# A state-space mixer in two blocks on one core: the order of GpSimd's two jobs in the decay matrix, and the slots of two exponentials

## The reference

```
z, xbc, dt = split(u @ w_in)
xbc = silu(dwconv(xbc, conv_w, conv_b)); xh, bm, cm = split(xbc)
# per chunk, for each of the two directions:
cum = cumsum(dt * a)
decay = exp(where(causal, cum[:, None] - cum[None], -inf))
y = einsum(cb * decay, xdt)                         # inside the chunk
y += einsum(c, state) * exp(cum)                    # from the chunks before
state = state * exp(cum[-1]) + einsum(b, xdt * tail)
# both directions and the skip, then
y = rmsnorm_per_group(y * silu(z)) @ w_out
```

## Time and profile before

| | us |
|---|---|
| median of 3 runs | 1842.42 |
| lowest, highest | 1839.36, 1845.85 |
| the profiled execution | 1839.35 |
| its span | 1837.6 |

### The profile page before, as it was taken

One profiled execution on the slowest core, in us unless ns is written; L12 is line 12 of the kernel. 1 busy time (PEld: TensorE's weight loads), 2 busy tenths in 40 slices (PEclk: granted clock), 3 DMA queues, 4 the chain that ended last, 5 costly groups with the idle time before them and its releaser, 6 DMA issues.

```text
span 1837.6 us, 20988 instructions
## 1 busy us (share of the span) xinstructions
PE 1703.0 (93%) x7944; PEld 1368.1 (74%) x7944; DVE 1107.7 (60%) x1520; ACT 842.0 (46%) x1365; POOL 362.3 (20%) x299
## 2 busy tenths in 40 slices
PE   6878898898887999999998899999999999999998
PEld 4766676686665768888776677888678778888886
DVE  6666666667576757574747666776655653434343
ACT  5655565465543453444445235446354442414232
POOL 0253434444354000000004401222120110000001
PEclk9989999999998999999999999999999999999999
DMA  3633443443321222222222223222323233333331
GB/s 103 177 118 96 116 130 103 126 114 103 93 72 48 81 58 80 70 72 78 69 59 85 68 65 74 63 68 80 102 81 104 83 89 102 93 98 98 93 102 69
DMA packets 260106, 164.58 MB, mean 90 GB/s; under 512 B 26909, under 2 KB 249286, under 8 KB 258982
## 3 DMA queue, kind: packets, MB, share of 16 engines
q1 hardware_dynamic: 260006, 163.25, 31.0%
HBM read 160.86 MB, written 2.36 MB: 89 GB/s over the span
## 4 chain that ended last, share of the span: by engine, by line
PE 65%; DVE 12%; issue 9%; ACT 6%; POOL 5%; DMA 2%; SPq 1%; ACTq 0%; POOLq 0%; DVEq 0%
PE stream L79 18%; PE stream L81 18%; PE stream L80 18%; ACT weights_hi L137 2%; DVE weights_lo L147 2%; POOL ssd_work L726 2%; PE q L775 1%; DVE ssd_x L980 1%; PE q L1962 1%; PE q L1986 1%; DMA ssd_exp_cum<-ssd_cum_pairs 1%; POOL ssd_work L730 1%; PE q L79 1%; PE q L81 1%; PE q L80 1%
## 5 line engine op out<-in xcount | busy, mean ns | idle before, releaser
L79 PE MATMUL stream<-u_lo,weights_hi 128*128 128x512 f32 (+2 forms) x1312 | 532.2, 406 | 11.5 <-DVE u_lo L249 4.5
L80 PE MATMUL stream<-u_hi,weights_lo 128*128 128x512 f32 (+2 forms) x1312 | 515.2, 393 | 0.0
L81 PE MATMUL stream<-u_hi,weights_hi 128*128 128x512 f32 (+2 forms) x1312 | 515.2, 393 | 0.0
L137 ACT ACTIVATE weights_hi<-weights_raw 128x1024 fp32r<-128x1024 f32 (+4 forms) x269 | 268.7, 1001 | 499.1 <-PE stream L81 473.1
L147 DVE TENSOR_TENSOR weights_lo<-weights_raw,weights_hi 128x1024 fp32r<-128x1024 f32 (+4 forms) x269 | 323.2, 1203 | 278.0 <-ACT weights_hi L137 277.7
L79 PEld LDWEIGHTS stream<-u_lo,weights_hi 128*128 128x128 f32 (+2 forms) x1312 | 248.2, 189 | 77.9 <-issue 9.3
L80 PEld LDWEIGHTS stream<-u_hi,weights_lo 128*128 128x128 f32 (+2 forms) x1312 | 247.9, 189 | 54.6 <-issue 4.9
L81 PEld LDWEIGHTS stream<-u_hi,weights_hi 128*128 128x128 f32 (+2 forms) x1312 | 247.4, 189 | 55.2 <-issue 0.7
L217 POOL COPY h_sum_of_squares<-h_squares 128x512 f32<-128x512 f32 x5 | 3.2, 649 | 795.3 <-ACT h_squares L205 795.3
L79 PE MATMUL stream<-ssd_y_lo,weights_hi 128*128 128x512 f32 x128 | 61.0, 477 | 45.2 <-DVE ssd_x L980 33.2
L79 PE MATMUL stream<-mlp_a_lo,weights_hi 128*128 128x512 f32 x256 | 100.2, 391 | 0.0
(11 more groups left out here) (460 smaller groups left out, 2925.6 us busy)
## 6 DMA issues: line engine op xcount, KB each, us to landing
weights_raw<-in_w_mlp_dram SPq DMA_DIRECT2D x64, 512.0 KB, 3.8
weights_raw<-in_ssd_w_in_dram SPq DMA_DIRECT2D x48, 512.0 KB, 4.1
weights_raw<-in_gla_w_in_dram SPq DMA_DIRECT2D x40, 512.0 KB, 3.8
ssd_cum_steps<-ssd_cum_rows SPq DMA_DIRECT2D x32, 512.0 KB, 4.9
weights_raw<-in_w_in_dram SPq DMA_DIRECT2D x29, 512.0 KB, 3.8
ssd_exp_cum<-ssd_cum_pairs SPq DMA_DIRECT2D x16, 512.0 KB, 7.6
weights_raw<-in_ssd_w_out_dram SPq DMA_DIRECT2D x16, 512.0 KB, 3.6
weights_raw<-in_gla_w_out_dram SPq DMA_DIRECT2D x13, 512.0 KB, 3.4
```

What stands on the lines that cost most here:

```text
L79: pe.matmul(out, lh, rl, start=first, stop=False, skip_group_check=skip)
L80: pe.matmul(out, ll, rh, start=False, stop=False, skip_group_check=skip)
L81: return pe.matmul(out, lh, rh, start=False, stop=last, skip_group_check=skip)
L137: act.activation(w_view(c, n)[0], raw_view(c, n), ACT.Copy).then_inc(c.w_rounded, 1)
```

## The change

POOL's joins get a table of their own, `JOIN`, one slot behind the cuts (for group 0: slots 0 and 1 of round 1; for the others slots 4, 5, 6 and 7). In a slot, the joins now stand behind the work; only in slot 7 do they stand ahead of `complete`. ACT's exponentials of the joined steps (`DECAY`) each come one slot later. The exponentials of `ex` move from slots 2 and 5 to slots 4 and 5. No instruction is added or taken away.

```diff
--- before.py
+++ after.py
@@ -598,12 +598,13 @@
         G = range(SG)
         CONV = {2: 0, 3: 1, 5: 2, 6: 3}
         CUT = {(0, 7): ((0, 0), (0, 1)), (1, 0): ((0, 2), (0, 3))}
-        DECAY = {(1, 0): ((0, 0), (0, 1)), (1, 1): ((0, 2), (0, 3))}
+        JOIN = {(1, 0): ((0, 0), (0, 1)), (1, 1): ((0, 2), (0, 3))}
+        DECAY = {(1, 1): ((0, 0), (0, 1)), (1, 2): ((0, 2), (0, 3))}
         for g in range(1, SG):
-            for t, cut, decay in ((0, (g, 3), (g, 4)), (1, (g, 4), (g, 5)), (2, (g, 5), (g, 6)),
-                                   (3, (g, 6), (g + 1, 0))):
-                CUT[cut] = CUT.get(cut, ()) + ((g, t),)
-                DECAY[decay] = DECAY.get(decay, ()) + ((g, t),)
+            for t, cut, join, decay in ((0, (g, 3), (g, 4), (g, 5)), (1, (g, 4), (g, 5), (g, 6)),
+                                        (2, (g, 5), (g, 6), (g + 1, 0)), (3, (g, 6), (g, 7), (g + 1, 1))):
+                for table, slot in ((CUT, cut), (JOIN, join), (DECAY, decay)):
+                    table[slot] = table.get(slot, ()) + ((g, t),)
 
         def conv_tile(g, j):
             return (2 * g, 2 * g + 1, 2 * SG + g, 3 * SG + g)[j]
@@ -700,17 +701,21 @@
                 pool.wait_ge(s_zsilu, g + 1)
                 pool.tensor_tensor(y[:, p, :], y[:, p, :], zs[:, g % 2, p, :], ALU.mult).then_inc(s_fin, 1)
 
+            def join_steps(i, k):
+                for pg, t in JOIN.get((i, k), ()):
+                    pool.wait_ge(s_cut, 4 * pg + t + 1)
+                    flat_steps = [steps[:, (4 * pg + t) % RING, d, :, :].rearrange("p h l -> p (h l)") for d in range(2)]
+                    pool.tensor_tensor(flat_steps[0], flat_steps[0], flat_steps[1], ALU.add).then_inc(s_join, 1)
+
             for i, k in slots:
                 g = i - 1
                 if k == 0 and i - 2 in G:
                     complete(i - 2, 1)
-                for pg, t in CUT.get((i, k), ()):
-                    pool.wait_ge(s_cut, 4 * pg + t + 1)
-                    flat_steps = [steps[:, (4 * pg + t) % RING, d, :, :].rearrange("p h l -> p (h l)") for d in range(2)]
-                    pool.tensor_tensor(flat_steps[0], flat_steps[0], flat_steps[1], ALU.add).then_inc(s_join, 1)
                 if g not in G:
+                    join_steps(i, k)
                     continue
                 if k == 7:
+                    join_steps(i, k)
                     complete(g, 0)
                 if 2 <= k <= 5:
 
@@ -728,6 +733,8 @@
                                            spread(head(dtc, d, t, g), P), ALU.mult).then_inc(s_t2, 1)
                     pool.wait_ge(s_t2, 3 * n + 2)
                     pool.tensor_tensor(ways[0], ways[0], ways[1], ALU.add).then_inc(s_t2, 1)
+                if k < 7:
+                    join_steps(i, k)
             c.second_mixer_set_up(pool, [(s_nrm, SG), (s_y, 4 * SG), (s_st, 7 * SG), (s_m, 4 * SG)])
             add_squares(c, pool)
 
@@ -874,8 +881,8 @@
                         scale_tile(c, act, nx, (pk - 4) // 3 * 4 + j, final)
                         square_tile(c, act, (pk - 4) // 3 * 4 + j, final)
 
-                if k in (2, 5) and g in G:
-                    p = (k - 2) // 3
+                if k in (4, 5) and g in G:
+                    p = k - 4
                     act.wait_ge(s_el, 32 * (g + 1))
                     act.activation(ex[:, 2 * p:2 * p + 2, :], ex[:, 2 * p:2 * p + 2, :], ACT.Exp).then_inc(s_ee, 1)
                 if k == 1 and g in G:
```

## The result

| | before | changed |
|---|---|---|
| median, us (runs) | 1843.74 (4) | 1793.93 (4) |
| lowest, highest | 1839.36, 1845.85 | 1793.04, 1795.42 |
| the profiled execution, its span | 1839.35, 1837.6 | 1795.42, 1793.7 |

The ratio is 0.9734, 95% interval 0.9713 to 0.9754: 2.7% faster, 49.8 us between the medians. The forecast was 1797, range 1784 to 1809. The two profiled executions are the fastest of before and the slowest of the changed kernel, so their difference, 43.9 us of span, is less than that of the medians. It is placed by markers: the transposes that open a round, the first product of the second mixer, and the end.

The account below looks back on a forecast made before the run. PE was taken to bound the kernel, held by its slot 4 wait for taps and the half clock after it. Gains of 36.6 + 5.7 + 2.9 = 45.2 us from 1839.35 gave 1794, or 1797 for a median; range 1784 to 1809.

Parts of the forecast that it names:

- The cause: Rounds 2 to 7, slot 4: PE waits 5.53 us for taps because POOL sleeps for join 0 before work 1.
- Slot 4, step by step: Rounds 2 to 7: PE's wait for taps 0.9 instead of 5.53 us; 6.1 gained per round, between 5.4 and 7.4.
- The rest of the round: Later slots of rounds 2 to 7: costed at nothing, bounds -0.5 to +0.5 us per round.
- The exponential's place: Rounds 2 to 7: leaving slot 2 only gives DVE slack, no gain or cost apart from delaying cut 1.
- what was feared for it in slot 4: The exponential ahead of cut 1 brings join 1 against DVE's cut of weights; whoever is second waits 1.1 to 1.2 us.
- Round 1: 3.4 us from PE going sooner and about 2.3 from the clock: 5.7 gained, between 3 and 8.
- The first part: Round 1, state's copy: PE goes at 94.5 instead of 97.91, 3.4 us sooner, idle 1.9 only.
- Round 8: ACT's wait of 2.97 us for the exponential's DMA goes: 2.9 gained, between 0 and 4.0.
- The clock: Rival, 14%: half rate returns in slot 4 and round 1, 16.1 us lost, 29 gained, 1813.
- The release: Rival, 5%: m 1 stood for something else, PE still waits 5.5 us, only round 8 gains; 1839.
- the slower rival: Rival, 4%: last chunk's steps, loaded behind DVE's cut of slot 4, reach ACT late in slot 6; 1859 us.
- strict sum, 32: Rounds 2 to 7, DVE second to POOL both times on the shared operands: 6 x 5.4 = 32 us gained.

Follow-up runs that it names:

- 7 repeats: The changed kernel with POOL's first product repeated 7 times ahead of work 1 in rounds 2 to 7: 1823.15 us.
- 11 and 13 repeats: The changed kernel with POOL's first product repeated 11 or 13 times ahead of work 1 in rounds 2 to 7: 1845.52 and 1859.46 us.

## Why the prediction held, and where it did not

**The cause** was right. POOL slept for join 0 in front of work 1, m 1 slept for work 1 in DVE's queue, and the taps behind it held PE's bank. The order alone gives 33.6 us; moving m 1 behind the taps removes the wait for taps with POOL untouched.

**Slot 4, step by step.** Forecast: m 1 behind join 0, the taps 0.9 late, close free 0.4 late, a gain of 6.5; or 5.4 if DVE's cut of weights comes second behind join 1. Measured: 0.81, 0.3 and 6.54 (before 13.03 us from the slot's third matmul to the state product, now 6.49). DVE won the race with join 1 by 0.05 us, so the value taken between the two, 6.1, was 0.4 low. (The middle of 6.5 and 5.4 is 5.95; 6.1 is more than rounding it up.) The kernel with the exponential behind the root, where POOL wins by 0.03, has the other branch: 1.0 per round more.

**The rest of the round** gave about 0.5 more, most of it in slots 5 to 7; what it is was not shown. The sum for rounds 2 to 7 was 36.6 and is 42.1.

**The exponential's place** was the step that failed. "In rounds 2 to 7 that only gives DVE slack ... No gain, no cost" was read from the old schedule, in which DVE idled behind y's rest anyway. With that idle time gone DVE's queue is full from the first x taps to slot 5, and what comes late at its head comes late at its end. The place is worth 2.2 us per round, 1.2 for being off the root's path and 1.0 for making cut 1 and join 1 later, the opposite sign of what was feared for it in slot 4. The second part fails in the old schedule too: there the move alone gave 1.2 per round by taking join 1 off m 1, whose 1.74 us in the earlier trace rows the prediction left unexplained. The sum was near only because the new waits had been worked out for the whole change, with y's rest on time as it is when the exponential is gone; credited separately, 13 us of rounds 2 to 7 were put down to the order that are the exponential's.

**Round 1** was mis-sized: 5.7 forecast, 3.8 measured. The first part came as forecast and better: PE's wait for the state's copy is 0.55 instead of 5.28. Then ACT's wait for steps did not shrink from 3.01 but grew to 6.51, since their load stands behind DVE's cut of slot 5, which came only 3.5 us sooner; PE's wait in slot 7 grew from 3.63 to 7.13. Loading them one unit earlier gives 3.3 of it back.

**Round 8** was mis-sized: 2.9 forecast, 1.3 measured. The output did start 2.50 sooner, as did everything up to 511.53. There PE was granted the half clock for the last tile and the norm's product, where before, after the same wait of 2.7, it had 1.00, and 1.6 went (0.4 of it came back further on).

**The total** was near in part by luck. From the same execution, 45.2 was forecast and 43.9 of span was measured: rounds 2 to 7 brought 5.5 more than their term, rounds 1 and 8 together 3.5 less, and 3.3 went in the stretches before and behind them, which no term covered. No term left its own bounds.

**The rivals.** The clock did not fall in slot 4; it did behind each wait of 4.36 us or more in that place, in the other kernels. The release was named rightly. Steps loaded behind DVE's cut did become late, as the slower rival had it, but only in round 1. The Trainium skill's rule on the shared operands ("SBUF — State Buffer", section "SBUF: two separate sides") was right in kind: every collision shown here is one after the other, as the cut of 1.22 us that took 2.34 beside a join of 1.29; none is shared. Its strict sum, 32, did not come, as DVE was first in one of the two.

## What to carry to other kernels

An in-order engine should not wait for next round's work in front of this round's; look for the longest idle time ahead of a short instruction and ask who queues behind. When a wait goes, read again every step that was free because of it: slack in the old schedule is no slack in the new. Once a queue is full, the order of two engines on a shared resource, decided by 0.03 to 0.05 us, is worth 1 us per round, and moving one party out of the stretch altogether is surer than timing it.

## What was not expected of the hardware

A DVE instruction with both inputs in SBUF and a POOL one take turns in every row shown: 0.69 became 1.76, 1.22 became 2.34, 1.29 became 2.31, each time by about the other's remaining length, while DVE's taps, with one input in PSUM, stayed at 3.09 to 3.11 for four beside POOL's joins and works. A POOL instruction that waits gets its turn between two DVE instructions that stand back to back: so join 0 came between y's rest and m 1.

PE's clock has two levels here, full (2.4 GHz) and half (1.2 GHz), and waits of the same length were followed by either. Over the six rounds of a kernel, the clock fell around the wait in none with 1.2 us (order alone); in none of six with 2.02 (joins in the same slot) but in two of six with 1.8 to 2.05 (7 repeats); in three of six with 2.98 (m 1 behind the taps); in six of six with 3.23 (m 1 behind close), with 4.36 (exponentials only), with 5.5 (before) and with 6.1 to 9.2 (11 and 13 repeats). In round 8 a wait of 2.7 was followed by the full level in the profile before and by the half one after. So a part of what a wait costs differs from round to round and from execution to execution: the 1.6 us of round 8, and the 3.3 us at 737 of the untouched stages. What decides it stays open.
